# Whole-row weight units, both accumulators open and a rearranged expert order in the gathered mixture-of-experts stage of a retention and convolution layer

## What is computed

```python
gates = ...                                   # 2 of 16 experts for each token
for e in range(N_EXPERTS):                    # 16
    he = jax.nn.silu(xt @ w_gate[e]) * (xt @ w_up[e])     # 1024 x 1024 each
    y = y + gates[:, e:e + 1] * (he @ w_down[e])          # 1024 x 1024
x = layernorm(alpha * x + y, ln2_g, ln2_b)
```

## Time and profile before

| | |
|---|---|
| median of 3 runs | 1305.79 us (1303.9 to 1307.8) |
| profiled execution | 1306.49 us, its span 1304.7 us |
| PE busy over the span | 1186.6 us (91%) |
| DVE, ACT busy | 996.3 us (76%), 632.8 us (48%) |
| the expert stage on PE | 699.2 to 1260.3 us, 16 experts |
| moved over the span | 332 MB, of which 264 MB on SP's queue |

### The profile page before, as it was taken

One profiled execution on the slowest core, in us unless ns is written; L12 is line 12 of the kernel. 1 busy time (PEld: TensorE's weight loads), 2 busy tenths in 40 slices (PEclk: granted clock), 3 DMA queues, 4 the chain that ended last, 5 costly groups with the idle time before them and its releaser, 6 DMA issues.

```text
span 1304.7 us, 15355 instructions
## 1 busy us (share of the span) xinstructions
PE 1186.6 (91%) x5825; PEld 909.9 (70%) x5825; DVE 996.3 (76%) x1301; ACT 632.8 (48%) x565; POOL 121.9 (9%) x216
## 2 busy tenths in 40 slices
PE   3999999999999999999736999999999999999960
PEld 3985986798589759998524767676767677676740
DVE  3598779778986986465644888888888888888846
ACT  2350324134122502453114777777777777777740
POOL 3111020112012011000030000000000000000012
PEclk9999999999999999999857999999999999999985
DMA  8565483466347545345345999999999999999934
GB/s 213 179 209 193 125 262 125 178 201 234 117 178 228 196 176 174 129 129 192 130 134 211 356 373 380 388 377 381 381 382 379 381 380 380 381 382 380 388 95 109
DMA packets 171052, 332.25 MB, mean 255 GB/s; under 512 B 8154, under 2 KB 45322, under 8 KB 170960
## 3 DMA queue, kind: packets, MB, share of 16 engines
q1 hardware_dynamic: 150576, 264.41, 57.9%
q0 software_dynamic: 20400, 66.81, 15.2%
HBM read 295.28 MB, written 36.63 MB: 254 GB/s over the span
## 4 chain that ended last, share of the span: by engine, by line
PE 84%; DVE 7%; DMA 3%; ACT 3%; issue 2%; POOL 2%; POOLq 0%; DVEq 0%; ACTq 0%
PE bank L676 77%; PE bank L888 4%; PE bank L717 3%; DMA v2rows<-in_b_conv_o_dram 1%; DVE o_tok L1360 1%; DMA x_slots<-x,slot 1%; DMA y_back<-y_slots,slot 1%; DVE sg_lo L1374 1%; DVE sg_f L1372 1%; POOL x_slots L633 1%; ACT sg_hi L1074 1%; DMA y_slots<-yo 0%; POOL vrows L520 0%; DVE stats L1351 0%; DVE lo L996 0%
## 5 line engine op out<-in xcount | busy, mean ns | idle before, releaser
L1516 DVE TENSOR_TENSOR mlo<-mraw,mhi 128x2048 fp32r<-128x2048 f32 x192 | 439.5, 2290 | 79.1 <-ACT mhi L1140 75.8
L1140 ACT ACTIVATE mhi<-mraw 128x2048 fp32r<-128x2048 f32 x192 | 367.5, 1915 | 93.8 <-PE bank L676 83.7
L676 PE MATMUL bank<-mhi,xg_hi 128*96 128x512 f32 x512 | 203.2, 397 | 1.4 <-DVE xg_lo L1521 1.4
L676 PE MATMUL bank<-mhi,xg_lo 128*96 128x512 f32 x512 | 203.0, 397 | 0.0
L676 PE MATMUL bank<-mlo,xg_hi 128*96 128x512 f32 x512 | 201.7, 394 | 0.0
L996 DVE TENSOR_TENSOR lo<-raw,hi 128x2048 fp32r<-128x2048 f32 x56 | 128.3, 2290 | 83.2 <-ACT hi L1103 38.7
L991 ACT ACTIVATE hi<-raw 128x2048 fp32r<-128x2048 f32 x47 | 90.0, 1914 | 191.4 <-PE bank L676 191.4
L676 PE MATMUL bank<-xT_hi,hi 128*128 128x336 f32 x512 | 165.3, 323 | 6.4 <-DVE lo L996 6.4
L676 PE MATMUL bank<-xT_hi,lo 128*128 128x336 f32 x512 | 163.1, 319 | 0.0
L676 PE MATMUL bank<-xT_lo,hi 128*128 128x336 f32 x512 | 163.0, 318 | 0.0
L1269 DVE SCALAR_TENSOR_TENSOR cT<-E,hv,cT 128x272 f32<-128x272 f32 x480 | 150.3, 388 | 0.0
(11 more groups left out here) (245 smaller groups left out, 1572.9 us busy)
## 6 DMA issues: line engine op xcount, KB each, us to landing
mraw<-in_w_gate_dram SPq DMA_DIRECT2D x64, 1024.0 KB, 11.2
mraw<-in_w_up_dram SPq DMA_DIRECT2D x64, 1024.0 KB, 11.1
mraw<-in_w_down_dram SPq DMA_DIRECT2D x64, 1024.0 KB, 11.9
raw<-in_w_in_dram SPq DMA_DIRECT2D x40, 1024.0 KB, 5.3
st<-in_state_ret_dram POOLq DMA_DIRECT2D x32, 512.0 KB, 4.8
out_dram<-st POOLq DMA_DIRECT2D x32, 512.0 KB, 3.9
raw<-in_w_ret_o_dram SPq DMA_DIRECT2D x8, 1024.0 KB, 7.1
x_slots<-zeros POOLq DMA_DIRECT2D x12, 512.0 KB, 4.7
```

What stands on the lines that cost most here:

```text
L676: i = pe.matmul(out, a, b, start=s, stop=e)
L1140: act.activation(mhi[:, v % MH, :], mraw[:, v % MR, :], ACT.Copy).then_inc(mhi_ready, 1)
L1516: dve.tensor_tensor(mlo[:, v % MH, :], mraw[:, v % MR, :], mhi[:, v % MH, :].bitcast(f32), ALU.subtract).then_inc(mlo_ready, 1)
```

## The change

- A unit is now two whole rows a partition. Partition p holds rows 8p to 8p+7 of the matrix and unit j takes rows 8p+2j and 8p+2j+1, 8 KB in one run.
- So a unit holds two contraction tiles of all 1024 columns: PE makes 6 matmuls into the accumulator of columns 0 to 511 and 6 into that of columns 512 to 1023, both open over the four units of a matrix. The transposes of `xg_tok` and `h_tok` take every eighth column, and `sgt` has two halves.
- An expert's units go g0 to g3, u0 to u3, d0 to d3, but units g0 and g1 of the next expert stand before d0 (`ORDER`).
- The 8 transposes of the next input stand between u1 and u2. The 8 transposes of the hidden rows stand between g0 and g1 of the next expert, or straight behind u3 for the last expert.
- ACT and DVE get the matching order. The experts are written out singly (`EXP`), the counter `turned` is gone, and POOL issues the load of the expert after next before it waits for a result.

```diff
-
+        ORDER = [(0, "g", 0), (0, "g", 1)]
+        for e in range(NE):
+            ORDER += [(e, "g", 2), (e, "g", 3)] + [(e, "u", j) for j in range(4)]
+            ORDER += [(e + 1, "g", 0), (e + 1, "g", 1)] * (e < NE - 1) + [(e, "d", j) for j in range(4)]
+        PLACE = {u: i for i, u in enumerate(ORDER)}
+
...
-            def pair_unit(v, it):
-                if v >= MR:
-                    sp.wait_ge(mlo_ready, U_PAIR.idx(v, it) + (MLEAD + 1 - MR))
+            def expert_unit(i):
+                e, kind, j = ORDER[i]
+                if i >= MR:
+                    sp.wait_ge(mlo_ready, i + MLEAD + 1 - MR)
                     alone(sp, waits_met)
-                more, v = divmod(v, 24)
-                p, u = divmod(v, 12)
-                w, n, half = ((w_gate, 0, u), (w_up, 0, u - 2), (w_gate, 1, u - 4), (w_up, 1, u - 6))[u // 2] if u < 8 else (w_down, u % 2, (u - 8) // 2)
-                e = it * 2 + (2 * more + p)
-                src = w[0][ds(e, 1)].rearrange("e (t p) n -> p (e t) n", p=128)
-                sp.dma_start(T_view(mraw, v % MR), src[:, 4 * half:4 * half + 4, 512 * n:512 * n + 512]).then_inc(mraw_full[v % MR], 16)
+                w = dict(g=w_gate, u=w_up, d=w_down)[kind]
+                sp.dma_start(mraw[:, i % MR, :], w[0, e].rearrange("(p j t) n -> p j (t n)", p=128, j=4)[:, j, :]).then_inc(mraw_full[i % MR], 16)
...
+                def tokens(e):
+
+                    pe.wait_ge(xg_full[e % 2], 16 * (e // 2 + 1))
+                    for j in range(2):
+                        b = bank[EXP.bank[f"xt{e}_{j}"]]
+                        turn(EXP, f"xt{e}_{j}", 0, [(b[:, i * CAP:(i + 1) * CAP], xg_tok[:, e % 2, 4 * j + i:D:8], CAP) for i in range(4)])
+
+                def hidden_turned(e):
+
+                    for n in range(2):
+                        evacuated(f"u{e}n{n}")
                     alone(pe, waits_met)
...
+                        name = f"{kind}{e}n{n}"
+                        if j == 0:
+                            room(EXP, name, 0)
+                        out = bank[EXP.bank[name]][0:CAP, :]
+                        cols = slice(512 * n, 512 * n + 512)
+                        mms = []
+                        for t in range(2):
+                            k = 2 * j + t
+                            mms += [(out, xh[:, k, :], wh[:, t, cols], k == 0, False), (out, xh[:, k, :], wl[:, t, cols], False, False),
+                                    (out, xl[:, k, :], wh[:, t, cols], False, k == KT - 1)]
+                        for o, a, b, st_, en in mms:
+                            last = pe.matmul(o, a, b, start=st_, stop=en)
+                        if j == 3 or n == 1:
+                            last.then_inc(group_done, 1)
+
+                tokens(0)
+                for j in range(2):
+                    evacuated(f"xt0_{j}")
+                unit(0, "g", 0)
+                unit(0, "g", 1)
+                for e in range(NE):
+                    more = e < NE - 1
+                    unit(e, "g", 2)
+                    unit(e, "g", 3)
+                    unit(e, "u", 0)
+                    unit(e, "u", 1)
+                    if more:
+                        tokens(e + 1)
+                    unit(e, "u", 2)
+                    unit(e, "u", 3)
+                    if more:
                         for j in range(2):
-                            evacuated(stage, f"xt0{j}", it)
-                    for u, name in ((0, f"g{p}0"), (2, f"u{p}0")):
-                        for kh in range(2):
-                            half(stage, v + u + kh, it, wit, name, kh, xh, xl)
-                    for kh in range(2):
-                        half(stage, v + 4 + kh, it, wit, f"g{p}1", kh, xh, xl)
-                    h_turn(stage, p, 0, it)
-                    if following:
+                            evacuated(f"xt{e + 1}_{j}")
+                        unit(e + 1, "g", 0)
+                    hidden_turned(e)
+                    if more:
+                        unit(e + 1, "g", 1)
+                    for j in range(2):
+                        evacuated(f"ht{e}_{j}")
+                    for j in range(4):
+                        unit(e, "d", j)
...
+                def hi_of(i):
+                    if i >= len(ORDER):
+                        return
+                    act.wait_ge(mraw_full[i % MR], (i // MR + 1) * 16)
+                    if i >= MH:
+                        act.wait_ge(group_done, EXP.done(unit_end(i - MH)))
+                    act.activation(mhi[:, i % MH, :], mraw[:, i % MR, :], ACT.Copy).then_inc(mhi_ready, 1)
...
+                    hi_of(at + 5)
+                    hi_of(at + 6)
+                    if e < NE - 1:
+                        turned_hi(f"xt{e + 1}_0", xg_hi[:, (e + 1) % 2, 0:4, :], xghi_ready)
+                    hi_of(at + 7)
+                    if e < NE - 1:
+                        turned_hi(f"xt{e + 1}_1", xg_hi[:, (e + 1) % 2, 4:8, :], xghi_ready)
+                    hi_of(at + 8)
+                    for j in range(2):
+                        turned_hi(f"ht{e}_{j}", hT_hi[:, 4 * j:4 * j + 4, :], hthi_ready)
...
+                for e in range(NE):
+                    at = PLACE[e, "g", 2]
+                    for i in range(3, 7):
+                        lo_of(at + i)
+                    if e < NE - 1:
+                        tokens_lo(e + 1, 0)
+                    lo_of(at + 7)
+                    if e < NE - 1:
+                        tokens_lo(e + 1, 1)
+                    hidden(e, 0)
+                    hidden(e, 1)
+                    lo_of(at + 8)
+                    for j in range(2):
+                        ks = slice(4 * j, 4 * j + 4)
+                        turned_lo(f"ht{e}_{j}", hT_lo[:, ks, :], hT_hi[:, ks, :], hthi_ready, 2 * e + j + 1)
+                    if e < NE - 1:
+                        for i in range(9, 15):
+                            lo_of(at + i)
+                    else:
+                        lo_of(at + 9)
                 for n in range(2):
-                    dve.wait_ge(*took(LAST, f"d1{n}"))
+                    dve.wait_ge(*took(EXP, f"d{NE - 1}n{n}"))
                 dve.sem_inc(moe_done, 1)
```

More of the change, by code:

```diff
@@ L720, in gathered_path @@
             def gathered_path():
[L721 to L739, removed]
-                    group(stage, name, it, mms)
@@ new lines, in unit @@
+                def unit(e, kind, j):
+                    i = PLACE[e, kind, j]
+                    pe.wait_ge(mlo_ready, i + 1 + MLEAD)
+                    xh, xl = (hT_hi, hT_lo) if kind == "d" else (xg_hi[:, e % 2], xg_lo[:, e % 2])
+                    wh, wl = (a[:, i % MH, :].rearrange("p (t n) -> p t n", t=2) for a in (mhi, mlo))
+                    for n in range(2):
+                        name = f"{kind}{e}n{n}"
[12 more added lines that the diff above has]
+                            last.then_inc(group_done, 1)
@@ L1132, in _ @@
             with act.If(act.value_load(most_i[0:1, 0:1], min_val=0, max_val=T) <= CAP):
-                def hi_of(v, stage, it, wit):
-                    act.wait_ge(mraw_full[v % MR], (wit * (24 // MR) + (v // MR + 1)) * 16)
-                    if v >= MH:
-                        act.wait_ge(group_done, stage.done(U_PAIR.last[v - MH], it))
-                    elif stage is not FIRST:
-                        act.wait_ge(group_done, stage.start(it))
-                    act.activation(mhi[:, v % MH, :], mraw[:, v % MR, :], ACT.Copy).then_inc(mhi_ready, 1)
@@ new lines, in turned_hi, with swish, result @@
+                def turned_hi(name, dst, ready):
+                    b, e_ = full(EXP, name)
+                    act.activation(dst, b[:, 0:4 * CAP].rearrange("p (k n) -> p k n", k=4), ACT.Copy).then_inc(ready, 1)
+                def swish(e, n):
+                    if e:
+                        act.wait_ge(*took(EXP, f"u{e - 1}n{n}"))
+                    b, e_ = full(EXP, f"g{e}n{n}")
+                    act.activation(sgt[:, n, :], b[0:CAP, :], ACT.Silu).then_inc(e_, 1)
+                def result(e, n):
+                    if n == 0:
+                        act.wait_ge(yo_free, e + 1)
+                    b, e_ = full(EXP, f"d{e}n{n}")
+                    act.activation(yo[:, e % 2, 512 * n:512 * n + 512], b[0:CAP, :], ACT.Copy).then_inc(e_, 1)
@@ L1551, in _ @@
-                lo_of(0, 0)
-                lo_of(1, 0)
-                for j in range(2):
-                    turned_lo(FIRST, f"xt{j}", 0, xg_lo[:, 0, 4 * j:4 * j + 4, :], xg_hi[:, 0, 4 * j:4 * j + 4, :], xghi_ready, j + 1)
-                for j in range(2):
-                    dve.wait_ge(*took(FIRST, f"xt{j}"))
-                dve.sem_inc(turned, 1)
-                for it in range(NE // 2 - 1):
-                    for p in range(2):
-                        expert(PAIR, p, it, it, True)
@@ new lines, in tokens_lo, with hidden @@
+                def tokens_lo(e, j):
+                    ks = slice(4 * j, 4 * j + 4)
```

(24 more changed lines are left out.)

182 lines of the change are left out of this document (54 added, 128 removed).

## The result

The changed kernel takes 1353.67 us (median of 4 runs, 1352.19 to 1357.28) against 1306.32 us before (4 runs), a ratio of 1.0368 with a 95% interval of 1.0341 to 1.0396. It is 47 us slower, 3.7%. Forecast were 1346.6 us and a range of 1338 to 1366.

The account below looks back on a forecast made before the run. PE was taken to bound the kernel. 34.8 (new waits) + 5.8 (last expert) + 2.0 (clock) - 1.8 (waits gone) = +40.8 us, forecast 1346.6 us; own range 1340 to 1352, full range 1338 to 1366.

Parts of the forecast that it names:

- What bounds the kernel: Expert stage: PE sets the pace, busy 99.56 of 100 us; nobody waits for a load.
- the rival of a shorter interval: PE's matmul interval falls from 0.2319 to 0.2133 us, saving 43 us, ending at about 1304; chance 0.03.
- the full cost of the step: Rival: transposes reading every eighth column take double, up to 19 us more, 1366 us; chance 0.22 for over 8 us.
- The wait that comes: PE waits for DVE's second `xg_lo` before the next expert's g0: 2.32 us at 15 experts, +34.8 us.
- The last expert: No next gate unit covers its hidden rows between u3 and d0: +5.8 us, plus 2 for a clock fall.
- Transposes with a step: Transposes' weight loads reading every eighth column: taken as 0, at most 19 us in all.
- The waits that go: PE's waits for turning hidden half 1 after one down unit vanish, covered by a gate unit: -1.8 us.
- The clock at the waits: Rival: PE's clock falls at each of the 15 waits, 2.2 us more each, 1380 us; chance 0.05.
- The loads: 8 KB runs cost 0 since nobody waits for a load; bound 4% less per busy time, 373 GB/s.

Follow-up runs that it names:

- tile rows: Changed kernel with each unit's two rows a partition taken 128 rows apart (two 4 KB runs), transposes reading columns in a row: 1353.67 us.
- `h_tok` split: Changed kernel with ACT's and DVE's second xg steps and DVE's first `h_tok` ahead of next g1's copy and subtraction: 1315.68 us; with two 4 KB runs 1311.82.

## Why the prediction was right

- **What bounds the kernel.** PE, and no load: right. Every edit moved the time by what it added to or took from PE's stream. The matmul interval stayed 0.23 us, so the rival of a shorter interval is out. The Trainium skill's figure for it (TensorE: Matmul & The Clock Gate, "Wait — 56ns, not 53.3ns?"), 0.2157 us, no run here shows: the median step from matmul to matmul is 0.231 or 0.232 us in every one, and that decides.
- **The time.** Forecast 1346.6 us, measured 1353.67, 7 us more. That is outside the forecast's own 1340 to 1352. It is inside 1338 to 1366 because this range was drawn up to the full cost of the step. The chain of waits, 40 of the 46 us, was right; what follows says which terms were mis-sized, and some of the errors cancel.
- **The wait that comes.** Forecast 15 times 2.32 us, 34.8 us; measured 2.29, 34.3 us. The chain held step for step. The wake-up of PE was 0.10 us here, not the 0.15 taken.
- **The last expert.** Forecast 5.8 us; measured 3.41 + 2.97 us less the usual 0.24 and 0.81, 5.3 us. PE's wake-up for the transposes was 0.25 us here (1290.01 to 1290.26). The clock's fall there came as forecast and cost seven slow steps, some 1.4 us, not 2.
- **Transposes with a step.** Here I took 0 and kept 19 as the end of the range. 8 transposes take 0.80 us in place of 0.61. That is 5.6 us over the stage (29.9 less 22.1, less the 2.2 of the last expert's wait in it): the mis-sized term. The nearest rows, were at a step of 2, and did not carry over to a step of 8. The Trainium skill (SBUF — State Buffer, Door 1: The DMA port swizzle, its note on 16-byte "cachelines") has reads at full rate with two in a line and a penalty below that. The traces agree in sign: weight loads take 196 against 189 ns at two to a line, and at one to a line those of the transposes take 203 ns in the kernel after against 140 before, a transpose 0.10 against 0.076 us. It is a third more a transpose, not the doubling that I kept as the bound.
- **The waits that go.** Forecast 1.8 us from the waits of the earlier trace rows, measured about 4: the steps into transposes took 11.4 us over 32, the usual 0.235 would be 7.5. In the view of waits only part shows, since records of matmuls overlap and a short wait hides under the end of the last one. The mis-sizing went the other way than the step's.
- **The clock at the waits.** I gave it 0.05 that it falls at each of them. It fell at 2 of 15, 6 of 15 with tile rows, and 15 of 15 at 5.7 us. As a yes or no the rival was badly put: for the changed kernel it cost 12 or so slow steps, 2.4 us, and each wait that restarts at full clock costs a further 0.06 us in its first matmul (0.29 for 0.23).
- **The sum.** 34.3 + 5.3 + 1.4 + 5.6 + 2.4 + 0.9 - 4.0 is 45.9 us, of 46.2 between the two spans. Against 40.8 forecast the step, the clock at the waits and the restarts are missing, 8.9 us; the waits that went were taken 2.2 too small, and the first three terms together 1.6 too large.
- **The loads.** Cost 0 was right. The bound, 4% less per busy time for larger pieces, pointed the wrong way: SP's queue moved the same bytes in less.

## What to carry to other kernels

When an order is rewritten, follow each value that the bounding engine waits for back through the other engines' queues, and count what stands ahead of it: an item that itself waits for the bounding engine (here the copy of the unit three ahead) makes a loop whose length must fit into the work that covers it, 5.1 us against 2.8 here. The cure was to move short steps ahead of a long one, here one on ACT and two on DVE. And a page that shows the DMA engines full says nothing of a gain from better loads while nobody waits for them.

## What the runs showed of the hardware

- PE's granted clock fell at some waits of 2.3 us and not at others of the same length in the same execution (2 of 15 in the kernel after, 6 of 15 with tile rows), fell at all 15 of 5.7 us, and came back after 5 to 13 steps of 0.43 us. With tile rows, taking 0.4 us an expert off the transposes gained nothing while the waits stood, and 3 to 4 us once they were gone.
- Reading fp32 columns 8 apart made a transpose of 96 x 128 a third slower (0.10 us against 0.076, start to start); its weight load took 203 ns against 140.
- Loads of 1 MB (down units) landed 11.9 us after issue in 2 KB runs and 7.4 us in 4 KB runs at the same pace of the kernel; with `h_tok` split, under 1% slower, 6.5 and 7.0 us in two executions with 8 KB runs and 7.6 with 4 KB. From 4 KB to 8 KB there is little left.
- The profile put PE's 15 waits at the next g0 down to "issue". The engine that ended them was found only by laying the timelines side by side, and shown by moving one instruction.
